# Two transformer blocks on one core: the first half of each layer of the second block in another order

## The chip, the cores and the metric

The kernel runs on 1 core of one Trainium2 chip. The metric is the device time of one execution in microseconds (us), lower is better. Time before: 3315.8 us, the median of 3 runs (3314.15 to 3320.59). Engines are named as in the profile: PE (TensorE), PEld (its weight loads), DVE (VectorE), ACT (ScalarE), POOL (GpSimd), SP (SyncE, which issues the DMAs).

## What is computed

The reference runs `first_block` (a token mixer and a mixture of experts, one layer) and then `second_block`, which has two layers. The change touches the first half of each of these two layers, for 256 tokens of width 1024 in float32:

```python
h = rmsnorm(x, norm_mix[l])
(dq, dk, dv, dz, db, da, sq, sk, sv, iq, ik, iw, xq, gl) = jnp.split(h @ w_in[l], split_pts, axis=-1)
o_dn = deltanet_branch(dq, dk, dv, dz, db, da, conv_w[l], a_log[l], dt_bias[l], dn_norm[l])
o_sa = dsa_branch(sq, sk, sv, iq, ik, iw, positions)
o_xa = memory_branch(xq, rmsnorm(mem, norm_mem[l]), w_mem_kv[l])
# deltanet_branch
qkv = jax.nn.silu(causal_conv(jnp.concatenate([q_in, k_in, v_in], axis=-1), conv_w))
o = gated_delta_rule(q, k, v, beta, g)
o = rmsnorm(o, dn_norm) * jax.nn.silu(z)
# dsa_branch: 8 heads, each query sees the 64 keys with the greatest index score
score = jnp.einsum('bths,bth->bts', jax.nn.relu(jnp.einsum('bthd,bsd->bths', iqb, ik)), iwb)
_, sel = lax.top_k(score, k_sel)
p = jax.nn.softmax(logits, axis=-1)          # over the selected keys
# memory_branch: 4 heads over 256 memory rows
p = jax.nn.softmax(logits, axis=-1)
```

## The kernel before

Every engine has its own program, written out by hand; semaphores tie them together. The two layers are one hardware loop of two rounds (`pe_layers`, `act_layers`, `vec_layers`, `pool_layers`, `sp_layers`).

**Weights.** A layer has 53 weight slabs of 2 MB (`LAY_SLABS`), loaded by SP in that order into three places, slab n into place n mod 3 once the slab before it there is used. Each slab is two halves. A half is split for fp32r products: ACT copies it rounded into a "high" buffer (L1638), DVE subtracts that in place (L1641). `Splitter.until(n, i)` says how far ahead ACT and DVE go: two halves past half i of slab n. The high buffers form rings of three places in SBUF (`RINGS`), so a half can be split only when PE has used the half three before it. PE uses a slab in 96 or 48 matmuls: `project_T` (result transposed, 96 of 256 columns) or `project` (48 of 512 columns), each product in three passes (L451, L452, L453). Results go to four PSUM banks that DVE empties (ring V) or four that ACT empties (ring A); a bank is opened again only when it was emptied.

**Order of the first half of a layer.** PE: 4 slabs of the memory's keys and values; `few` with 16 columns; memory queries xq (slabs 4, 5); the memory's logits (L1830); sq and sk (6 to 9); per memory head a turn of the probabilities (`probs_to_T`, L1806) and the values (L1845); index queries iq (10); `few` with 72 columns; sv (11, 12); transposes of sq, sk, iq, ik; index scores (L1866); six slabs dq, dk, dv of the DeltaNet branch (13 to 18), whose 12 half results ("pairs") ACT copies into `raw` (L2193); own attention: logits of 4 heads (L1876), per head a turn (L1806) and the values (L1898), then the other 4 heads and the norms of q and k by columns of ones (`norms`: L1886, L1890); the DeltaNet solve and the recurrence over 4 chunks (L1920 to L2000); two slabs z (19, 20); gates and branch products (21 and on).

**Convolution.** A pair is convolved in place over its 4 taps: pairs 0 to 8 by DVE (`convolve`, L2469, L2471), one after the split of each slab's half together with one of 8 rounds of taking the 8 greatest scores (L2480 to L2486); pairs 9, 10, 11 by POOL (L2710 to L2715), two blocks each. ACT takes the Silu of the pairs in the order 0 to 11 (L2200), each after a wait for its convolution, and then the exponentials of own attention (`probs`, L2126), which DVE normalises (`normalise`, L2374, L2376).

**After the recurrence.** DVE sums the squares of the result, signals `bgate_free`, POOL takes the power, DVE multiplies by it, by the gain and by Silu(z) (L2592 to L2594) and signals `od_ready`, for which PE waits before it transposes these rows. SP's program, in its queue's order, is: load of slab 21, wait for `bgate_free` (L1699), a DMA of the gate bias (L1700), load of slab 22:

```python
half_spent(sp, l, FIRST[follows(n) + 1] - 1)
load(n, l)
if kind == "in" and at >= GL0 and (at - GL0) % D == 0:
    sp.wait_ge(S("bgate_free"), 3 * l + BRANCHES.index(i) + 1)
    sp.dma_start(bgate, ...)
```

## Time and profile before

| | before |
|---|---|
| median of 3 runs | 3315.8 us |
| profiled execution | 3315.45 us |
| its span in the trace | 3313.6 us |
| PE busy | 2946.2 us (89%) |
| PE weight loads busy | 2303.4 us (70%) |
| DVE busy | 1872.7 us (57%) |
| ACT busy | 1456.6 us (44%) |
| POOL busy | 102.0 us (3%) |
| read from HBM | 608.46 MB |
| mean granted PE clock | 0.940 |

The median, the profiled execution and its span lie within 2.2 us of each other. Busy times are shares of the whole; what the change is worth is read from the stages that it touches. PE counts as busy also where its clock is granted at half speed, so a stage is read by three numbers: its length, PE's idle time and the granted clock.

### The profile page before, as it was taken

What the parts mean: (1) busy time and instruction counts of PE and PEld (TensorE: products, weight loads), DVE (VectorE), ACT (ScalarE), POOL (GpSimd) and SP (SyncE); (2) the same over time, 40 slices, a digit from 0 to 9 for tenths busy, and PEclk for the clock granted to TensorE, in tenths of its full rate; (3) what the DMA queues carried; (4) which work ended last, traced back from release to release, by engine and by line L of the source; (5) the groups of instructions that cost most, each with busy time, mean ns of one, the idle gap of its engine ahead of it and who ended that gap; (6) DMA issues with size and microseconds to landing.
All of it is one profiled execution on the core that took longest, in us unless ns stands there. A gap on an engine that the chain in (4) does not pass through costs nothing.

```text
span 3313.6 us, 41552 instructions
## 1 busy us (share of the span) xinstructions
PE 2946.2 (89%) x15389; PEld 2303.4 (70%) x15389; DVE 1872.7 (57%) x2190; ACT 1456.6 (44%) x1471; POOL 102.0 (3%) x156
## 2 busy tenths in 40 slices
PE   7999898789899989889896799989998958999897
PEld 1345444567666666658786698879797857988896
DVE  1113223788888898885457337545543664365454
ACT  1121111577777777763443435434334333353342
POOL 0000000000000000000004000000000050000000
PEclk9999999899999999998988799989999877999999
DMA  7420331798989888973423004534533320045354
GB/s 295 153 108 26 146 132 52 282 355 341 358 341 355 339 353 341 347 304 140 152 102 128 1 1 153 197 143 161 205 135 127 125 105 1 1 165 209 140 181 181
DMA packets 57721, 611.55 MB, mean 185 GB/s; under 512 B 12603, under 2 KB 18243, under 8 KB 21220
## 3 DMA queue, kind: packets, MB, share of 16 engines
q1 hardware_dynamic: 57574, 609.53, 48.5%
q8 instruction: 99, 1.62, 0.2%
q14 instruction: 48, 0.39, 0.0%
HBM read 608.46 MB, written 1.05 MB: 184 GB/s over the span
## 4 chain that ended last, share of the span: by engine, by line
issue 49%; PE 27%; DVE 9%; DMA 7%; ACT 4%; POOL 3%; DVEq 0%; SPq 0%; POOLq 0%; ACTq 0%
DVE arena_rounded L1225 7%; PE psum_scalar L461 6%; DMA weight_slabs<-in_expert_slabs 5%; PE psum_vector L461 4%; ACT arena_rounded L1222 3%; PE psum_vector L498 3%; PE psum_vector L1278 2%; PE psum_vector L1235 2%; POOL arena L2712 1%; PE psum_scalar L1265 1%; PE psum_scalar L1266 1%; PE psum_vector L451 1%; PE psum_vector L453 1%; PE psum_vector L452 1%; POOL arena L2715 1%
## 5 line engine op out<-in xcount | busy, mean ns | idle before, releaser
L1641 DVE TENSOR_TENSOR weight_slabs_rounded<-weight_slabs,arena_rounded 128x2048 fp32r<-128x2048 f32 x208 | 475.0, 2292 | 484.3 <-ACT arena_rounded L1638 470.3
L1225 DVE TENSOR_TENSOR arena_rounded<-weight_slabs,arena_rounded 128x2048 fp32r<-128x2048 f32 x290 | 651.8, 2288 | 60.1 <-ACT arena_rounded L1222 48.7
L1222 ACT ACTIVATE arena_rounded<-weight_slabs 128x2048 fp32r<-128x2048 f32 x290 | 548.1, 1912 | 128.7 <-DMA weight_slabs<-in_expert_slabs 62.5
L1638 ACT ACTIVATE arena_rounded<-weight_slabs 128x2048 fp32r<-128x2048 f32 x208 | 396.1, 1913 | 405.4 <-PE psum_vector L453 236.3
L451 PE MATMUL psum_vector<-arena_rounded,arena_rounded 128*128 128x512 f32 (+3 forms) x1136 | 404.5, 356 | 28.1 <-DVE weight_slabs_rounded L1641 17.2
L451 PE MATMUL psum_scalar<-arena_rounded,arena_rounded 128*128 128x256 f32 (+1 forms) x1248 | 389.9, 312 | 15.0 <-DVE weight_slabs_rounded L1641 12.1
L1265 PE MATMUL psum_scalar<-arena_rounded,arena_rounded 128*128 128x512 f32 x768 | 320.4, 417 | 74.8 <-DVE arena_rounded L1225 68.5
L1266 PE MATMUL psum_scalar<-arena_rounded,arena_rounded 128*128 128x512 f32 x768 | 304.5, 396 | 0.0
L453 PE MATMUL psum_vector<-arena_rounded,arena_rounded 128*128 128x512 f32 (+2 forms) x784 | 302.5, 386 | 0.0
L452 PE MATMUL psum_scalar<-arena_rounded,arena_rounded 128*128 128x256 f32 x992 | 285.4, 288 | 0.0
L453 PE MATMUL psum_scalar<-arena_rounded,weight_slabs_rounded 128*128 128x256 f32 x992 | 285.0, 287 | 0.0
L452 PE MATMUL psum_vector<-weight_slabs_rounded,arena_rounded 128*128 128x512 f32 x720 | 283.1, 393 | 0.0
L451 PEld LDWEIGHTS psum_scalar<-arena_rounded,arena_rounded 128*128 128x128 f32 x1248 | 245.5, 197 | 28.2 <-ACT small L1477 10.7
L451 PEld LDWEIGHTS psum_vector<-arena_rounded,arena_rounded 128*128 128x128 f32 x1136 | 219.3, 193 | 59.9 <-DVE weight_slabs_rounded L1641 26.5
L1265 PEld LDWEIGHTS psum_scalar<-arena_rounded,arena_rounded 128*128 128x128 f32 x768 | 145.7, 190 | 154.8 <-DVE arena_rounded L1225 127.7
L452 PEld LDWEIGHTS psum_scalar<-arena_rounded,arena_rounded 128*128 128x128 f32 x992 | 195.5, 197 | 0.0
L453 PEld LDWEIGHTS psum_scalar<-arena_rounded,weight_slabs_rounded 128*128 128x128 f32 x992 | 195.3, 197 | 0.0
L461 PE MATMUL psum_scalar<-weight_slabs,arena 128*128 128x512 f32 x416 | 184.7, 605 | 11.7 <-DMA weight_slabs<-in_mixer_slabs 11.7
L453 PEld LDWEIGHTS psum_vector<-arena_rounded,arena_rounded 128*128 128x128 f32 x784 | 152.0, 194 | 29.1
L1309 PE MATMUL psum_vector<-arena_rounded,arena_rounded 128*128 128x512 f32 x384 | 158.3, 412 | 12.3 <-DVE arena_rounded L1225 9.6
L1266 PEld LDWEIGHTS psum_scalar<-arena_rounded,arena_rounded 128*128 128x128 f32 x768 | 146.5, 191 | 26.9
L461 PEld LDWEIGHTS psum_scalar<-weight_slabs,arena 128*128 128x128 f32 x416 | 80.3, 195 | 112.7 <-issue 100.7
(440 smaller groups left out, 4315.1 us busy)
## 6 DMA issues: line engine op xcount, KB each, us to landing
weight_slabs<-in_expert_slabs SPq DMA_DIRECT2D x145, 2048.0 KB, 8.9
weight_slabs<-in_layer_slabs SPq DMA_DIRECT2D x103, 2048.0 KB, 7.8
weight_slabs<-in_mixer_slabs SPq DMA_DIRECT2D x32, 2048.0 KB, 7.9
weight_slabs<-in_layer_slabs SPq DMA_DIRECT2D x6, 1024.0 KB, 5.4
arena<-in_mem SPq DMA_DIRECT2D x3, 1024.0 KB, 9.8
arena<-in_b_gate SPq DMA_DIRECT2D x6, 512.0 KB, 8.1
constants<-in_constants SPq DMA_DIRECT2D x1, 1024.0 KB, 4.9
arena<-in_x SPq DMA_DIRECT2D x1, 1024.0 KB, 7.0
```

Source lines behind the costliest of these rows:

```text
L451: pe.matmul(out, left[0], right[0], start=start, stop=False)
L452: pe.matmul(out, left[0], right[1], start=False, stop=False)
L453: return pe.matmul(out, left[1], right[0], start=False, stop=stop)
L461: mm = pe.matmul(bank[:, :n], hT[:, k, t * P:(t + 1) * P], w[:, k, :n], start=k == 0, stop=k == chunks - 1)
L498: mm = pe.matmul(bank[0:2, :], c2s[:, :, k], w[:, k, :], start=k == 0, stop=k == KC - 1)
L1222: e.activation(high_, whole, ACT.Copy).then_inc(S("expert_high"), 1)
L1225: e.tensor_tensor(low, whole, high_.bitcast(F32), ALU.subtract).then_inc(S("expert_split"), 1)
L1265: pe.matmul(bank, xgT[:, k, :], high[:, k % 4], start=k == 0, stop=False)
L1266: mm = pe.matmul(bank, xgT[:, k, :], low[:, k % 4], start=False, stop=k == KC - 1)
L1309: pe.matmul(banks[side], actT[:, k, :], high[:, k % 2, cols], start=k == 0, stop=False)
L1638: e.activation(fr(high), low, ACT.Copy).then_inc(S("weights_high"), 1)
L1641: e.tensor_tensor(fr(low), low, fr(high).bitcast(F32), ALU.subtract).then_inc(S("weights_split"), 1)
```

## The change

The slabs come in another order, and with them the work of every engine:

- Index queries are slab 4, memory queries 5 and 6, sq 7 and 8, sk 9 and 10, dq/dk/dv 11 to 16, sv 17 and 18; z stays 19 and 20 but is multiplied before the recurrence. Both `few` come together. Index scores are made before sq.
- `take_greatest` (the round of 8) now runs four times beside slabs 9 and 10 and four times beside slabs 12 to 15.
- Convolution: pairs 0, 2, 4, 6, 8 to 11 by DVE, pairs 1, 3, 5, 7 by POOL from pair 1 on. ACT takes the Silus between the copies of later slabs, and all squares of q and k before own attention.
- Own attention: logits of 4 heads, one z slab (in the first group the norms stand between its halves), then turns and values; the same for the other 4 heads. The turns of two heads come ahead of the values.
- The power of Silu(z) is taken once, from SBUF. sq and sk are kept by heads; sq and qT, sk and kT share their places, and other rings are used. SP's program is unchanged but for the slabs' order.

```diff
-LAY_SLABS = ([("mem", BANK * n) for n in range(4)] + [("in", XQ0 + BANK * n) for n in range(2)]
+LAY_SLABS = ([("mem", BANK * n) for n in range(4)] + [("in", IQ0)] + [("in", XQ0 + BANK * n) for n in range(2)]
              + [("in", SQ0 + BANK * n) for n in range(2)] + [("in", SK0 + BANK * n) for n in range(2)]
-             + [("in", IQ0)] + [("in", SV0 + BANK * n) for n in range(2)]
-             + [("in", DQ0 + BANK * n) for n in range(6)] + [("in", DZ0 + BANK * n) for n in range(2)])
+             + [("in", DQ0 + BANK * n) for n in range(6)] + [("in", SV0 + BANK * n) for n in range(2)]
+             + [("in", DZ0 + BANK * n) for n in range(2)])
...
-        RINGS = {0: (112, 120, 48), 13: (72, 80, 24), 19: (48, 56), 21: (48, 56, 136), 35: (112, 120, 88)}
+        RINGS = {0: (112, 120, 48), 11: (112, 120, 24), 19: (112, 120, 96), 21: (48, 56, 136), 35: (112, 120, 88)}
...
-        PAIRS_V = 9
+        BY_VECTOR, BY_POOL = (0, 2, 4, 6, 8, 9, 10, 11), (1, 3, 5, 7)
...
-                ahead = 1 if n in (19, 20) else 2
-                last = min(FIRST[n] + min(i, FIRST[n + 1] - FIRST[n] - 1) + ahead, self.stop - 1)
+                last = min(FIRST[n] + min(i, FIRST[n + 1] - FIRST[n] - 1) + 2, self.stop - 1)
...
+                def own_logits(g):
+                    for h in range(4 * g, 4 * g + 4):
+                        bank = V.open()
+                        for t in range(NT):
+                            mm = pe.matmul(bank[:, t * T:(t + 1) * T], qT[:, h, t * P:(t + 1) * P], kT[:, h, :],
+                                           start=True, stop=True)
+                        V.close(mm)
...
+                V.close(few(V.open(), 16, 72, P))
+                project(V, hT)
                 project_T(A, hT)
...
+                pe.wait_ge(S("index_roped"), l + 1)
+                rows_to_T(pe, A, iq, chunks=4)
+                bank = A.open()
+                for t in range(NT):
+                    mm = pe.transpose(bank[:, t * P:(t + 1) * P], ik[:, t, :], ident)
+                A.close(mm)
                 project_T(A, hT)
+                pe.wait_ge(S("iqT_ready"), l + 1)
+                for h in range(IDXH):
...
+                project(A, hT)
+                probs_to_T(0)
+                probs_to_T(1)
+                project(A, hT)
+                for h in range(XH):
+                    memory_values(h)
+                    if h < 2:
+                        probs_to_T(h + 2)
+                for n in range(6):
+                    project_T(A, hT)
+                    if n == 2:
+                        pe.wait_ge(S("roped"), l + 1)
+                        heads_to_T(sq)
+                        heads_to_T(sk)
+                    own_logits(g)
+                    project(A, hT, norms if g == 0 else None)
+                    at = XH + 4 * g
+                    probs_to_T(at)
+                    probs_to_T(at + 1)
+                    for h in range(4):
+                        own_values(4 * g + h)
+                        if h < 2:
+                            probs_to_T(at + h + 2)
...
-                for n in range(2):
-                    project(A, hT)
...
+                def silu(j):
+                    if j in BY_VECTOR:
+                        e.wait_ge(S("conv_by_vector"), len(BY_VECTOR) * l + BY_VECTOR.index(j) + 1)
                     else:
-                        e.wait_ge(S("conv_by_pool"), (24 - 2 * PAIRS_V) * l + 2 * (j - PAIRS_V) + 2)
+                        e.wait_ge(S("conv_by_pool"), 2 * len(BY_POOL) * l + 2 * BY_POOL.index(j) + 2)
                     step(e.activation(raw[:, 2 * j:2 * j + 2, :], raw[:, 2 * j:2 * j + 2, :], ACT.Silu))
                     e.sem_inc(S("conv_ready"), 1)
+                SILU_AFTER = {2: (0,), 3: (1, 2), 4: (3, 4), 5: (6,)}
+                for n in range(6):
+                    for i in range(2):
+                        weights.until(11 + n, i)
+                        j = 2 * n + i
+                        A.give(e.activation(raw[:, 2 * j:2 * j + 2, :], A.take(), ACT.Copy), wait=True)
+                        e.sem_inc(S("raw_ready"), 1)
+                    if n == 2:
+                        copies([qT[:, k:k + 2, :] for k in range(0, KC, 2)] + [kT[:, k:k + 2, :] for k in range(0, KC, 2)])
+                        signal("qkT_ready")
+                    for j in SILU_AFTER.get(n, ()):
+                        silu(j)
+                for n in range(2):
+                    weights.until(17 + n)
+                    for t in range(NT):
+                        A.give(e.activation(sv[:, t, n * BANK:(n + 1) * BANK], A.take(), ACT.Copy))
+                    for j in ((5, 8, 9), (7, 10, 11))[n]:
+                        silu(j)
+                for part, squared_ in enumerate((q_squares, k_squares)):
+                    for j in range(0, H2, 2):
+                        step.go(e.activation(squared_[:, j:j + 2, :], raw[:, H2 * part + j:H2 * part + j + 2, :], ACT.Square))
+                step.sync()
+                e.sem_inc(S("squares_ready"), 1)
...
                     for h in range(4 * g, 4 * g + 4):
+                        if h % 2 == 0:
+                            weights.until(19 + g, h % 4 // 2)
+                        e.wait_ge(S("rmax_ready"), 12 * l + XH + h + 1)
                         probs(h, 1.0)
+                    for t in range(NT):
+                        A.give(e.activation(zrow[:, t, g * BANK:(g + 1) * BANK], A.take(), ACT.Copy))
+                    prob_turned(4 * g)
+                    prob_turned(4 * g + 1)
                     for h in range(4 * g, 4 * g + 4):
                         A.give(e.activation(osT[:, h, :], A.take()[:, 0:T], ACT.Copy))
+                        if h % 4 < 2:
+                            prob_turned(h + 2)
...
+                weights.upto(FIRST[21] + 1)
+                A.given()
+                step(e.activation(zrow, zrow, ACT.Silu))
+                e.sem_inc(S("z_ready"), 1)
...
+                for i in range(2):
+                    weights.until(10, i)
+                    take_greatest()
...
+                for n in range(4):
+                    weights.until(12 + n, 0)
+                    convolve(BY_VECTOR[n])
+                    weights.until(12 + n)
+                    take_greatest()
                 step(ts(barred, work, -2e38, NEG, ALU.is_gt, ALU.mult))
+                for n in range(2):
+                    for i in range(2):
+                        weights.until(16 + n, i)
+                        convolve(BY_VECTOR[4 + 2 * n + i])
+                weights.until(18)
...
+                own_greatest(0)
+                for h in range(4):
+                    if h == 2:
+                        weights.until(19, 0)
+                    normalise(h, XH + h)
...
-                for b in range(2 * PAIRS_V, 24):
+                for b in [2 * j + i for j in BY_POOL for i in range(2)]:
...
```

The new order on the engines, as a listing of their programs has it (in brackets the semaphores that an instruction waits for).

ACT before, after the last copies of the six DeltaNet slabs (L2193): Silus (L2200), then the exponentials (L2126).

```order
L2193 ACTIVATE arena<-psum_scalar 128x512 [waits lay_scalar_free,lay_scalar_full]
...
L2200 ACT_TABLE_LOAD
L2200 ACTIVATE arena<-arena 128x512 [waits conv_by_vector]
...
L2200 ACTIVATE arena<-arena 128x512 [waits conv_by_pool]
L176 REGISTER_ALU
L2199 REGISTER_ALU [waits lay_scalar_step]
L2200 ACTIVATE arena<-arena 128x512 [waits conv_by_pool]
...
L2126 ACT_TABLE_LOAD
L2126 ACTIVATE arena,small<-arena,small 128x256 [waits rmax_ready]
```

ACT now, from the end of the DeltaNet slabs (L2259 are its copies, L2269 those of sv, L2251 Silus, L2274 squares, L1639 high copies).

```order
L2259 ACTIVATE arena<-psum_scalar 128x512 [waits lay_scalar_full]
...
L2251 ACTIVATE arena<-arena 128x512 [waits lay_scalar_free,conv_by_pool]
...
L2269 ACTIVATE arena<-psum_scalar 128x512 [waits lay_scalar_full] x2
L2250 REGISTER_ALU
L2251 ACTIVATE arena<-arena 128x512 [waits conv_by_pool]
...
L2251 ACTIVATE arena<-arena 128x512 [waits conv_by_vector]
...
L2274 ACTIVATE arena<-arena 128x512 [waits lay_scalar_step]
L2274 ACTIVATE arena<-arena 128x512 x7
...
L2163 ACTIVATE arena,small<-arena,small 128x256 [waits rmax_ready]
```

The Silus moved between copies; the wait for POOL's last pair (7) now stands behind the copies of sv and ahead of the squares.

PE before, at the second group of own attention (L1876 logits, L1886 and L1890 norms, L1806 a turn, L1898 values).

```order
L1876 MATMUL psum_vector<-arena 128x256
L200 REGISTER_ALU [waits g_ready,squares_ready]
L1886 MATMUL psum_vector<-constants,arena 128x1 [waits lay_vector_free]
...
L1890 MATMUL psum_vector<-small,constants 128x8 x4
L1893 REGISTER_ALU
L200 REGISTER_ALU [waits prob_ready]
L1806 MATMUL psum_scalar<-constants,arena 128x128 [waits lay_scalar_free]
```

PE now, at the first group, between the halves of z slab 19 (L1858 and L1863 norms).

```order
L453 MATMUL psum_scalar<-arena_rounded_66,arena_rounded_53 128x512
L200 REGISTER_ALU [waits g_ready,squares_ready]
L1858 MATMUL psum_vector<-constants,arena 128x1 [waits lay_vector_free]
...
L1863 MATMUL psum_vector<-small,constants 128x8 x4
L1723 REGISTER_ALU
L451 MATMUL psum_scalar<-arena_rounded_67,arena_rounded_54 128x512 [waits weights_split]
```

A z slab's matmuls now stand between the logits and the first turn.

ACT now, behind the recurrence's copies (L2335); before, the copies of z stood here and the high copies of slabs 20 and 21 between them.

```order
L2335 ACTIVATE arena<-psum_scalar 64x512 [waits lay_scalar_full]
L228 REGISTER_ALU
L2338 ISA [waits lay_scalar_free]
L1635 REGISTER_ALU [waits bgate_free]
L1639 ACTIVATE arena_rounded_69<-weight_slabs 128x2048 [waits lay_slab1]
```

The first half that ACT prepares here is now slab 22's (place 1), where it was slab 20's.

## Rows read from the trace of the kernel before

**Rows 1.** The page: busy time per engine, granted clock in 40 slices.

```profile
PE 2946.2 (89%) x15389; PEld 2303.4 (70%) x15389; DVE 1872.7 (57%) x2190; ACT 1456.6 (44%) x1471; POOL 102.0 (3%) x156
...
PEclk9999999899999999998988799989999877999999
```

**Rows 2.** Waits of PE, first layer, 1553.2 to 1877.9: total, times, longest.

```profile
PE psum_scalar L1806 <- DVEq L2378: 40.4, 2, 36.2
PE psum_scalar L1898 <- ACTq L2214: 12.4, 8, 6.7
PE psum_scalar L1845 <- ACTq L2174: 5.1, 4, 2.6
```

**Rows 3.** Timeline, all engines, about the longest wait: start, duration, [idle before <- releaser].

```profile
1776.03 2.29 DVE L1641 TENSOR_TENSOR weight_slabs_rounded<-weight_slabs,arena_rounded 128x2048 fp32r<-128x2048 f32 x1
1777.84 0.53 POOL L2706 TENSOR_TENSOR arena<-halves 128x1 f32<-128x1 f32 x1 [263.57 <-ACTq L2194]
...
1786.24 0.19 POOL L2710 TENSOR_TENSOR small<-halves 128x1 f32<-128x1 f32 x1 [0.18 <-POOL arena L2715]
...
1802.36 0.19 POOL L2710 TENSOR_TENSOR small<-halves 128x1 f32<-128x1 f32 x1 [0.18 <-POOL arena L2715]
...
1816.88 0.19 POOL L2710 TENSOR_TENSOR small<-halves 128x1 f32<-128x1 f32 x1 [0.18 <-POOL arena L2715]
...
1823.17 0.72 POOL L2715 TENSOR_TENSOR arena<-arena 128x256 f32<-128x256 f32 x1
1823.97 0.63 ACT L2200 ACTIVATE arena<-arena 128x512 f32<-128x512 f32 x1 [13.82 <-POOLq L2716]
...
1827.23 0.17 DVE L2374 RECIPROCAL small<-small 128x2 f32<-128x2 f32 x1 [15.72 <-ACTq L2129]
...
1828.24 1.11 PE L1806 MATMUL psum_scalar<-constants,arena 128*128 128x128 f32 x4 [36.17 <-DVEq L2378]
```

**Rows 4.** Windows: length, busy (instructions) of PE, PEld, DVE, ACT, POOL, then PEclk, DMA.

```profile
1553.20:1788.40 235.20, 220.79 (x1355) 199.13 (x1354) 129.79 (x240) 91.86 (x103) 9.74 (x16) 0.93 0.37 135
1788.40:1878.00 89.60, 41.05 (x180) 34.06 (x179) 36.21 (x92) 31.20 (x70) 32.26 (x52) 0.62 0.06 24
...
1997.80:2020.00 22.20, 22.08 (x97) 17.94 (x96) 12.91 (x12) 9.51 (x9) 2.93 (x1) 1.00 0.33 119
...
2453.00:2690.00 237.00, 223.04 (x1347) 201.24 (x1347) 129.58 (x239) 91.36 (x103) 9.48 (x16) 0.91 0.37 134
2690.00:2780.00 90.00, 41.45 (x180) 33.92 (x180) 36.46 (x93) 31.19 (x70) 32.55 (x52) 0.60 0.07 24
```

**Rows 5.** Windows: own attention after the long wait; DeltaNet slabs; after a late pause.

```profile
1828.20:1878.00 49.80, 37.39 (x162) 31.17 (x163) 14.41 (x42) 18.46 (x50) 0.00 (x0) 0.63 0.00 1
...
1740.00:1780.00 40.00, 40.00 (x336) 40.00 (x335) 33.77 (x67) 15.68 (x13) 2.01 (x5) 1.00 0.48 170
...
2150.00:2205.00 55.00, 41.58 (x198) 35.29 (x197) 28.18 (x35) 17.41 (x15) 0.70 (x1) 0.84 0.36 134
```

**Rows 6.** Groups of DVE, 1733 to 1777 (POOL idle): count | busy, mean ns.

```profile
L1641 DVE TENSOR_TENSOR weight_slabs_rounded<-weight_slabs,arena_rounded 128x2048 fp32r<-128x2048 f32 x9 | 20.6, 2292 | 5.5 <-ACT arena_rounded L1638 4.8
L2471 DVE SCALAR_TENSOR_TENSOR arena<-arena,small 128x254 f32<-128x254 f32 (+2 forms) x24 | 10.5, 481 | 0.4
```

**Rows 7.** The same, 1784.9 to 1802.55 (POOL convolving beside it).

```profile
L2471 DVE SCALAR_TENSOR_TENSOR arena<-arena,small 128x254 f32<-128x254 f32 (+2 forms) x18 | 9.9, 590 | 0.3
```

**Rows 8.** Waits and timeline of the DMA queue on SP, 1780 to 2010.

```profile
SPq L1699 <- DVEq L2584: 212.2, 1, 212.2
...
2001.68 0.33 SPq L1700 DMA_DIRECT2D arena<-in_b_gate  x1
2009.25 34.14 SPq L1658 DMA_DIRECT2D weight_slabs<-in_layer_slabs  x4
```

**Rows 9.** The page: ACT's high copy in the layers, and a slab's load.

```profile
L1638 ACT ACTIVATE arena_rounded<-weight_slabs 128x2048 fp32r<-128x2048 f32 x208 | 396.1, 1913 | 405.4 <-PE psum_vector L453 236.3
...
weight_slabs<-in_layer_slabs SPq DMA_DIRECT2D x103, 2048.0 KB, 7.8
```

368 lines of the change are left out of this document (176 added, 192 removed).

## The prediction

> **What bounds the kernel now.** I read the page first: PE is busy for 89% of the span at a mean clock of 0.94, and the slices in which both fall are two, one in each layer of the second block [rows 1]. Then the waits of PE over one layer's first half: of 64 us idle one wait is 36.2 us, that of the first turn of own attention for DVE's normalised probabilities [rows 2]. Then the timeline behind that wait, read backwards [rows 3]: PE starts at 1828.24, behind DVE's normalising at 1827.23, behind ACT's exponentials, which follow ACT's last Silu at 1823.97; that Silu waited 13.8 us for POOL, whose last add is at 1823.17. POOL began only at 1777.84, when pair 9 was there, and had six blocks to do. So a wait that is booked on DVE is POOL's convolution, handed on by ACT's fixed order. Last the windows [rows 4], to see what the stage is worth. The part up to the last DeltaNet slab takes 235.2 us with 220.8 busy at clock 0.93; own attention takes 89.6 us with 41.1 busy at 0.62; the two z slabs, behind the recurrence, take 22.2 us at full clock without a pause. The second layer reads the same: 237.0, 223.0 at 0.91, and 90.0, 41.5 at 0.60.
>
> **The ledger.** The change moves work within these 235.2 + 89.6 + 22.2 = 347.0 us per layer and takes none of PE's work away: the same matmuls are issued. So I count losses against PE's work. Before: idle 235.2 - 220.8 = 14.4 and 89.6 - 41.1 = 48.6; slow clock 0.07 x 220.8 = 15.5 in the first part, and 0.37 x 37.4 = 13.8 behind the long wait, where the clock is 0.63 [rows 4, 5]. That is 92 us lost, and 255 us of work per layer at full clock. Everything hangs on what is lost afterwards.
>
> **The change, part by part**, with T0 the start of the first DeltaNet slab and T the end of sv. A slab takes 96 x 40.0 / 336 = 11.4 us transposed and 22.2 / 2 = 11.1 us by rows [rows 4, 5]; T is T0 + 6 x 11.4 + 4 for the transposes of sq and sk + 22 = T0 + 95.
>
> - *Index scores and both small products early.* Same instructions. The score of a head costs an ACT copy and two DVE operations, and PE has four banks for eight heads, so it waits about 2 us; the next slab goes to the other ring, so DVE's sums are hidden behind sq. The memory's values find their banks behind ACT's copies of sk, about 2 us more. With turns of two heads ahead, the waits per memory head (5.1 us) [rows 2] should be nearly gone. Idle: 4 taken; 2 at the least, 14.4 as before at the most. The clock is granted slow after thin matmuls and after such waits; I take 12 of the 15.5, between 5 and 15.5.
> - *DVE in the DeltaNet slabs.* Before, one slab cost it two splits, a convolution and a round of eight: 33.8 us busy in 40 at PE's full pace [rows 5], 9.6 per slab of 11.4. Slabs 12 to 15 carry just that now, but with POOL beside them: the taps took 481 ns alone and 590 ns beside POOL [rows 6, 7], which adds 0.7 per pair, and a wait of up to 0.9 per split. That is 12.1 at the most, 0.7 over. Slabs 16 and 17 have two convolutions and no round, 4.6 + 2 x 4 to 2 x 4.5, so up to 2.2 over each. Lag 7 at the worst, against a lead of two halves (11.4) less copy and split (1.9 + 2.3), which is 7 [rows 6, 9]. I take 3; 0 and 12 are the ends.
> - *POOL.* It now has eight blocks, from T0 + 11.5. A block took (1802.36 - 1786.24) / 2 = 8.1 us beside DVE's taps and (1816.88 - 1802.36) / 2 = 7.3 later [rows 3]. No split ran beside it but one: POOL's first operation, 1777.84 to 1778.37, lasted 0.53 where its like takes 0.19, and ended 0.05 after the split that ran from 1776.03 to 1778.32. So I let a split hold POOL, for some 1.8 us, twice a slab: POOL works 7.8 us in 11.4, a block takes 8.1 x 11.4 / 7.8 = 11.8, and pair 7 is done at T0 + 106 = T + 11. Unheld it would be T0 + 76.
> - *Own attention.* ACT takes Silu 7 at T + 11, then pairs 10 and 11 and eight squares (0.6 each): squares ready at T + 18. PE does the logits (to T + 3.6), waits 1 us for z's first half, whose high buffer is that of sv's last half, and is through it at T + 10. It waits 8 us for the squares, does 9 us of norms (my estimate) and z's second half. The softmax of four heads (by my estimate 12 us through DVE and ACT, with two high copies between) is hidden behind these. Then turns and values, twice; before they cost 12.4 us of waits [rows 2], 6.7 of them for ACT's first copy behind its squares; 4 taken. The second group's softmax is covered by logits and z slab, 14.7. Idle 1 + 8 + 4 = 13, between 5 and 35; if POOL ends by T the 8 are gone. Clock: the norms' thin matmuls and the pause were slow before, 13.8; I take 12, between 5 and 15.
> - *z moved ahead.* Its 22.2 us are in the ledger. But they covered something. SP may not load slab 22 before `bgate_free`, which came at 2001.68, 3.9 us after the recurrence's last matmul [rows 8, 4]; before, slabs 19, 20 and 21 lay ready by then. Now only 21 does, 11.1 us of work, to 2008.9 on the old times. Slab 22 is issued at 2002, lands at about 2010.5 (7.8 us, behind the bias) [rows 9], is copied (1.9) and split (2.3): ready at 2014.8, PE waits 6. Behind that the first branch slab's split stands behind DVE's work on the DeltaNet rows and the first gate sums: 3. A late pause costs clock too (0.84 over 55 us around two waits) [rows 5]: 3. Tail: 12, between 4 and 22, z's whole length.
> - One Silu of z from SBUF, the rope by heads, fewer table changes: hidden in ACT and DVE, 0; if their cover goes it is the lag above.
>
> Sum of losses: 4 + 12 + 3 + 13 + 12 = 44, and 12 in the tail. Gain 92 - 44 - 12 = 36 per layer, 72 for both. The profiled execution took 3315.45, which is the median (3315.8) within 0.4. **Forecast: 3315.5 - 72 = 3243 us.** About 0.2% is what a measurement of this kernel can tell from no change.
>
> **The rivals.**
>
> - *The losses are smaller*: POOL is not held, so the squares are early; slab 22 comes in time; the clock stays up. Losses 28, tail 12 gives 52 per layer, **3211**; with a tail of 5 as well, 3197. For it: DVE's work beside POOL slowed POOL's blocks only from 7.3 to 8.1. Against: the one split seen beside POOL did hold it.
> - *DVE becomes the bound* of the DeltaNet slabs, lag 12 for 3: 27 per layer, **3261**. For it: 84% busy there already, and one of its operations is slower beside POOL. Against: two halves of lead.
> - *POOL is held by every operation of DVE's in turn*, not by splits alone: of a block's seven operations each waits for what DVE has in hand. With 0.5 us for each of seven taps and the two splits, a block comes to about 15 us, pair 7 to T0 + 131, and PE waits 25 us longer: 11 per layer, **3293**. Against: with DVE busy over 80% with taps and rounds, a block took 8.1. The Trainium skill's page "SBUF — State Buffer", section "Who interferes with whom", states this lock: VectorE and GpSimd share a port pair, an operation of VectorE with two SBUF inputs contends with a GpSimd read, and whichever starts second is blocked until the first ends. By that rule the trace agrees on the split that held POOL; it also speaks against sharing the convolution between these two engines over the whole DeltaNet stage.
> - *Slower than before*: the same chain, longer. ACT's order is fixed: behind the wait for pair 7 stand the squares, the exponentials and the high copies that PE needs. The gain of 36 is used up when pair 7 is 36 us later, at T0 + 142, a block of (142 - 11.5) / 8 = 16.3 us, twice what was measured. At 18.5 us a block the wait is 54 longer, 18 per layer lost, **3351**. Against it: while PE stands still DVE runs out of splits, and POOL catches up.
> - *The change doesn't do what it says*: the order of the programs shows z between logits and turns and the pairs shared; I leave this nothing of its own.
>
> **How the numbers follow.** Forecast 0.54, smaller losses 0.22, DVE 0.12, POOL held in turn 0.08, slower 0.04. All but the last are faster by over 0.2% (7 us); I move 0.02 from POOL's case and 0.01 from DVE's to no change: faster 0.93, same 0.03, slower 0.04. The bounds of single terms (clock 5 to 15 in each part, tail 4 to 22) move the forecast by some 20 per layer either way if several go together. The range leaves out the far half of the smaller losses and the slower case: 3205 to 3290.
>
> **What would show it.** Right: no wait of PE over 12 us in a layer's first half; POOL busy from the second pair on, its last add within 15 us of the end of sv; PE's wait before the norms 5 to 10 us; between first DeltaNet slab and the end of sv some 100 us; after the recurrence a wait of about 6 us before slab 22, for a split whose load was issued behind the gate bias. Wrong: waits for splits of 3 us or more all through the DeltaNet slabs (DVE's case), blocks of POOL of 15 us (held in turn), or a granted clock near 0.6 again in own attention, which would say that the pauses were only cut into pieces.

## The result, and the profile after

| | before | changed |
|---|---|---|
| median | 3315.7 us (4 runs, 3314.15 to 3320.59) | 3219.4 us (4 runs, 3212.26 to 3227.25) |
| ratio | | 0.9708, 95% interval 0.9682 to 0.9734 |
| profiled execution, span | 3315.45, 3313.6 | 3216.56, 3214.7 |
| mean granted PE clock | 0.940 | 0.956 |

The kernel is 2.9% faster, 96 us. The forecast was 72 (3243 us); the time lies inside the range, on its fast side. The page of the changed kernel, the rows that answer to [rows 1]:

```profile
PE 2932.7 (91%) x15389; PEld 2301.2 (72%) x15389; DVE 1873.0 (58%) x2162; ACT 1458.6 (45%) x1473; POOL 173.7 (5%) x200
...
PEclk9999999799999999999899899989998999999999
```

The work is the same, 15389 matmuls. POOL has eight blocks per layer for six and is busy 72 us longer in all, and nobody waits longer for it. No slice of the layers stands at clock 0.7 any more. Now the windows, to be held against [rows 4]; columns as there. They are the first narrow product to the end of sv, own attention with both z slabs, the DeltaNet solve and recurrence, and slabs 21 and 22 with 16 transposes up to the start of slab 23, all in the first layer; then the first two for the second layer:

```profile
1554.20:1781.80 227.60, 218.05 (x1356) 198.38 (x1355) 146.33 (x266) 98.25 (x112) 77.84 (x89) 0.95 0.38 139
1781.80:1840.90 59.10, 56.08 (x275) 47.98 (x274) 28.41 (x59) 34.12 (x69) 0.00 (x0) 0.88 0.10 36
1840.90:1963.30 122.40, 116.20 (x985) 112.78 (x982) 55.08 (x95) 49.65 (x92) 0.00 (x0) 0.97 0.01 1
1963.30:1997.10 33.80, 26.05 (x115) 21.04 (x113) 20.25 (x16) 14.43 (x12) 2.93 (x1) 0.90 0.57 217
...
2404.00:2635.00 231.00, 221.49 (x1374) 201.50 (x1373) 147.23 (x267) 101.09 (x114) 77.84 (x89) 0.96 0.38 139
2635.00:2692.00 57.00, 53.98 (x268) 46.34 (x267) 27.80 (x60) 31.99 (x70) 0.00 (x0) 0.88 0.07 31
```

The last two stretches of the first layer in the kernel before, the DeltaNet part and the end of the z slabs to the start of slab 23:

```profile
1878.00:1997.80 119.80, 115.64 (x984) 112.16 (x982) 53.18 (x93) 46.49 (x90) 0.00 (x0) 0.99 0.01 1
2019.90:2044.40 24.50, 23.69 (x113) 19.77 (x113) 21.37 (x18) 14.81 (x11) 0.00 (x0) 1.00 0.50 178
```

What took 347.0 us takes 227.6 + 59.1 = 286.7, which is 60.3 less. Two stretches give some of that back. Slabs 21 and 22 with their transposes took 24.5 us and take 33.8, 9.3 more. The DeltaNet part took 119.8 us and takes 122.4, 2.6 more: its first wait, for the factors, is 5.0 us for 2.6. That is 60.3 - 9.3 - 2.6 = 48.4 us per layer, and twice that is 96.8, against the 98.9 by which the spans differ. The ledger closes within about 2 us.

The waits of PE, 1553 to 1841, to be held against [rows 2]:

```profile
PE psum_scalar L451 <- ACT arena L2154: 5.1, 1, 5.1
PE psum_scalar L1817 <- ACT arena L2238: 2.6, 1, 2.6
PE psum_scalar L451 <- DVE weight_slabs_rounded L1642: 2.3, 3, 1.0
PE psum_vector L1858 <- ACTq L2276: 1.3, 1, 1.3
PE psum_scalar L1837 <- ACTq L2229: 0.8, 2, 0.4
PE psum_scalar L451 <- ACT arena L2228: 0.4, 1, 0.4
```

Instead of 64 us there are 12.5. The waits of the turns and values, 12.4 + 5.1 = 17.5 us before, have come down to the rows of L1817, L1837 and L2228, 3.8. The wait for the squares (L1858), for which the forecast had 8, is 1.3. New at the top is a wait of 5.1 for ACT at L2154. The timeline of all engines at the squares shows why POOL costs nothing:

```profile
1779.49 0.84 POOL L2824 TENSOR_TENSOR arena<-arena 128x256 f32<-128x256 f32 x1
...
1781.86 3.71 ACT L1639 ACTIVATE arena_rounded<-weight_slabs 128x2048 fp32r<-128x2048 f32 x2 [10.29 <-PE psum_scalar L453]
...
1786.43 0.63 ACT L2251 ACTIVATE arena<-arena 128x512 f32<-128x512 f32 x1
...
1788.75 4.28 ACT L2274 ACTIVATE arena<-arena 128x512 f32<-128x512 f32 x8
...
1793.20 3.73 PE L1858 MATMUL psum_vector<-constants,arena 128*128 128x1 f32 x32 [1.27 <-ACTq L2276]
```

POOL's last add ends at 1780.33. ACT comes for that pair (L2251) only at 1786.43: it stood for 10.29 us for PE's last sv slab and then had two high copies to make. So POOL is done 6 us before it is asked for.

### The profile page after: what moved, and what is told of

Its sections match the earlier page's. It is cut to its first block, busy times and chain, and to the rows that moved or that the text cites. A ratio compares the mean times of both kernels' runs of the same rounds, so it can differ in the third digit from the quotient of the medians.

```text
span 3214.7 us, 41574 instructions
## 1 busy us (share of the span) xinstructions
PE 2932.7 (91%) x15389; PEld 2301.2 (72%) x15389; DVE 1873.0 (58%) x2162; ACT 1458.6 (45%) x1473; POOL 173.7 (5%) x200
## 4 chain that ended last, share of the span: by engine, by line
issue 45%; PE 30%; DVE 9%; DMA 7%; POOL 5%; ACT 4%; DVEq 0%; SPq 0%; POOLq 0%; ACTq 0%
DVE arena_rounded L1225 7%; PE psum_scalar L461 6%; DMA weight_slabs<-in_expert_slabs 5%; PE psum_vector L461 4%; ACT arena_rounded L1222 3%; PE psum_vector L498 3%; PE psum_vector L1278 2%; POOL arena L2821 2%; PE psum_vector L1235 2%; PE psum_scalar L1265 2%; POOL arena L2824 2%; PE psum_scalar L1266 1%; PE psum_vector L451 1%; PE psum_vector L453 1%; PE psum_vector L452 1%
## 5 line engine op out<-in xcount | busy, mean ns | idle before, releaser
L1642 DVE TENSOR_TENSOR weight_slabs_rounded<-weight_slabs,arena_rounded 128x2048 fp32r<-128x2048 f32 x208 | 478.4, 2308 | 419.9 <-ACT arena_rounded L1639 403.2
L1639 ACT ACTIVATE arena_rounded<-weight_slabs 128x2048 fp32r<-128x2048 f32 x208 | 396.2, 1913 | 451.2 <-PE psum_vector L453 260.0
L451 PE MATMUL psum_vector<-arena_rounded,arena_rounded 128*128 128x512 f32 (+3 forms) x1136 | 411.1, 362 | 41.5 <-DVE weight_slabs_rounded L1642 31.2
L451 PEld LDWEIGHTS psum_vector<-arena_rounded,arena_rounded 128*128 128x128 f32 x1136 | 224.5, 198 | 75.7 <-DVE weight_slabs_rounded L1642 41.2
L451 PEld LDWEIGHTS psum_scalar<-arena_rounded,arena_rounded 128*128 128x128 f32 x1248 | 243.4, 195 | 45.2 <-ACT arena L2154 10.6
L453 PEld LDWEIGHTS psum_vector<-arena_rounded,arena_rounded 128*128 128x128 f32 x784 | 156.6, 200 | 29.8
```

The source lines that it names most:

```text
L451: pe.matmul(out, left[0], right[0], start=start, stop=False)
L453: return pe.matmul(out, left[1], right[0], start=False, stop=stop)
L1639: e.activation(fr(high), low, ACT.Copy).then_inc(S("weights_high"), 1)
L1642: e.tensor_tensor(fr(low), low, fr(high).bitcast(F32), ALU.subtract).then_inc(S("weights_split"), 1)
```

## The experiments

All are edits of the changed kernel. Six undo or worsen parts of the change, to see what each is worth (1 to 6); three take away one wait each that is left, and one has these together (7 to 10); two are about the clock (11, 12). Ratios are to the kernel before, with 95% intervals; the changed kernel stands at 0.9708, and 0.001 of ratio is 1.66 us per layer.

**1. POOL starts late again (pool_last).**

```diff
-        BY_VECTOR, BY_POOL = (0, 2, 4, 6, 8, 9, 10, 11), (1, 3, 5, 7)
+        BY_VECTOR, BY_POOL = (0, 1, 2, 3, 4, 5, 6, 7, 8), (9, 10, 11)
```

ACT's Silus follow this order, and DVE takes its ninth pair (8) behind the splits of the last sv slab.

> Edit of the changed kernel: POOL takes pairs 9, 10 and 11 of the convolution (as before the change) and VectorE pairs 0 to 8; everything else stays in the new order. Theory A (the gain is a sum of parts; sharing the convolution from its second half-slab on is one of them): POOL starts some 44 us later, at the tenth pair, and has 6 blocks of 7 to 10.4 us, so it ends 41 to 62 us after that, 12 to 23 us behind the end of the last sv slab instead of 1.5 us ahead of it. The squares come 12 to 20 us later, TensorE waits for them ahead of the norms for 13 to 21 us instead of 1.3, and the kernel takes 12 to 20 us more per layer, 24 to 40 in all (3243 to 3259). Rival 1 (the split of the convolution carries nearly the whole gain): about 45 us per layer, over 3300. Rival 2 (the softmax of the own attention hides POOL anyway): under 5 us per layer, below 3230.

Measured: 3261.04 us, ratio 0.9840 (0.9822 to 0.9857), 22 us more per layer, just above the 20 expected. The first layer, timeline about the squares:

```profile
1804.04 0.72 POOL L2825 TENSOR_TENSOR arena<-arena 128x256 f32<-128x256 f32 x1
1804.84 0.63 ACT L2251 ACTIVATE arena<-arena 128x512 f32<-128x512 f32 x1 [11.81 <-POOLq L2826]
1805.59 4.26 ACT L2274 ACTIVATE arena<-arena 128x512 f32<-128x512 f32 x8
1810.03 6.98 PE L1858 MATMUL psum_vector<-constants,arena 128*128 128x1 f32 x32 [20.20 <-ACTq L2276]
```

The chain of [rows 3] is back: POOL, a Silu of ACT that waits 11.8 us for it, the squares, and PE, which waits 20.2 instead of 1.3. The 32 narrow products behind that wait take 6.98 us where they took 3.73: the rest of the 22 us is clock. Sharing from the first pairs on carries almost half the gain, by removing this chain; rivals 1 and 2 fall.

**2. POOL made slower (pool_plus).**

```diff
                         step.go(e.tensor_tensor(unused, halves[:, 0:1], halves[:, 0:1], ALU.mult))
+                        if tap == 2:
+                            step(e.tensor_scalar(slack[:, 0, late:T], raw[:, b, 0:T - late], tap_column(tap, b), None, ALU.mult))
+                            step.go(e.tensor_tensor(unused, halves[:, 0:1], halves[:, 0:1], ALU.mult))
```

> Edit of the changed kernel: each of POOL's eight blocks gets one more multiplication of 255 columns (its result goes to a cell that nobody reads) and one more of its small dummy operations, about 1.65 us per block, 13 us per layer. Theory A (POOL now ends 1.5 us ahead of the sv slabs, ScalarE comes for its last pair 4.6 us behind their end): POOL ends about 11.7 us behind the sv slabs, the last silu and all squares come 7 us later, TensorE waits for them about 8 us instead of 1.3, and the kernel takes 5 to 9 us more per layer, 10 to 18 in all (3229 to 3237). Rival (POOL's end is still covered, as own logits and the first half of a z slab lie before the norms): under 2 us per layer. Rival 2 (POOL is the bound now, all of its added time shows): 13 us per layer, 3245.

Measured: 3235.7 us, ratio 0.9763 (0.9747 to 0.9779), 9 us more per layer. POOL's last add ends 11.1 us behind the start of the own logits instead of 1.3 ahead of it, and ACT now waits for it:

```profile
1793.94 0.72 POOL L2828 TENSOR_TENSOR arena<-arena 128x256 f32<-128x256 f32 x1
1794.74 0.63 ACT L2252 ACTIVATE arena<-arena 128x512 f32<-128x512 f32 x1 [6.28 <-POOLq L2829]
...
1801.49 6.98 PE L1859 MATMUL psum_vector<-constants,arena 128*128 128x1 f32 x32 [7.53 <-ACTq L2277]
```

Of 12.4 us by which POOL ends later, 6.3 are on PE's path and 6 were slack; with the clock behind it the step costs 9. So POOL has a slack of 6 us, behind which each us costs more than one. This is the mechanism of the "slower than before" case, at the point where it begins.

**3. The z slabs behind own attention (z_behind).**

```diff
                     own_logits(g)
-                    project(A, hT, norms if g == 0 else None)
+                    if g == 0:
+                        norms()
...
+                for g in range(2):
+                    project(A, hT)
+
                 def tile(t):
```

> Edit of the changed kernel: the two z slabs are multiplied between the own attention and the DeltaNet recurrence instead of between each group's logits and its turns; the norms keep their place after the first group's logits. Theory A: in the first group the norms themselves (11 to 14 us) cover the softmax, but TensorE gets to them 6 to 8 us before the squares and waits that long; in the second group nothing covers it: four heads of 1.86 us on VectorE, an exponential and a division, 8 to 10 us of waiting. With 2 to 4 us of half clock that is 15 to 22 us per layer, 30 to 44 in all (3249 to 3263). Rival 1 (z slabs are the whole gain): 45 us per layer, over 3300. Rival 2 (groups of four are enough by themselves): under 5 us per layer.

Measured: 3249.27 us, ratio 0.9802 (0.9784 to 0.9821), 15.6 us more per layer. The waits of PE in the same stretch:

```profile
PE psum_vector L1858 <- ACTq L2280: 7.9, 1, 7.9
PE psum_scalar L1817 <- DVEq L2457: 5.8, 1, 5.8
```

The z slabs' copies on ACT move with them. Both waits stand where theory A put them, 7.9 us ahead of the norms and 5.8 in the second group. The second was expected at 8 to 10 and is smaller. They are 12.4 us more than in the changed kernel, the waits for z's first split and the first values 1.7 less; the other 5 are clock: turns that take 1.0 us there take 2.0 here.

**4. Turns directly ahead of the values (turns_late).**

```diff
-                    probs_to_T(at)
-                    probs_to_T(at + 1)
                     for h in range(4):
+                        probs_to_T(at + h)
                         own_values(4 * g + h)
-                        if h < 2:
-                            probs_to_T(at + h + 2)
```

and the same for the memory's heads and for ACT's order.

> Edit of the changed kernel: in the memory and the own attention each head's probabilities are turned directly before its values again, not two heads ahead, and ScalarE's copies follow that order. Theory A: TensorE then waits 0.8 to 1.3 us for ScalarE's copy at each of the 12 heads, 10 to 15 us per layer, 20 to 30 in all (3239 to 3249). Rival (other work on ScalarE set these times already): no difference over 5 us in all.

Measured: 3247.05 us, ratio 0.9803 (0.9785 to 0.9821), 15.7 us more per layer, just over the band. The waits:

```profile
PE psum_scalar L1828 <- ACTq L2223: 7.8, 4, 5.2
PE psum_scalar L1837 <- ACTq L2223: 6.6, 8, 0.9
```

Eleven heads wait 0.8 to 0.9 us each. One waits 5.2: the first of the memory, because ACT, at the end of the second sk slab, first makes two high copies (3.7 us) and the two copies of sk (1.1 us). That is 10.6 us more of waits, and 5 of clock. Turning ahead is worth as much as the z slabs.

**5. All three at once (undone).**

> The edits of three runs together: POOL takes the last three pairs, the z slabs follow the own attention, and turns stand directly ahead of their values. What is left of the change is the early index scores, the order of the slabs, the groups of four and the transposes in place. Alone, the three cost 0.0132, 0.0094 and 0.0095 of the time before. Theory A (each part pays for a wait of its own at its own place: the squares, the second group's softmax, the copy of the turned probabilities): they add up, 0.999 to 1.006 of the time before, which is the whole gain and a little more. Rival 1 (they cover one and the same chain of the own attention, so that the second undone costs less): 0.980 to 0.992. Rival 2 (the early index scores and the new order carry a gain of their own, so that even this kernel is faster than before by over 0.5 per cent).

Measured: 3330.38 us, ratio 1.0051 (1.0035 to 1.0068): 0.5% slower than before the change. The single ratios add up to 0.9708 + 0.0132 + 0.0094 + 0.0095 = 1.0029, and the three add up within the intervals. The waits of PE, first layer:

```profile
PE psum_vector L1858 <- ACTq L2271: 26.9, 1, 26.9
PE psum_scalar L1828 <- ACTq L2227: 7.7, 4, 5.2
PE psum_scalar L1837 <- ACTq L2227: 6.5, 8, 0.8
PE psum_scalar L1817 <- DVEq L2445: 5.1, 1, 5.1
```

Each wait is the one of its own run (L1817 is 5.1 for 5.8), and the first is the sum of two: 1.3 + 18.9 (late POOL) + 6.6 (z no longer ahead of the norms) = 26.8. And the windows of the same two parts (here both z slabs are within the second):

```profile
1554.20:1787.00 232.80, 219.97 (x1344) 199.59 (x1344) 140.28 (x266) 95.84 (x108) 29.63 (x36) 0.93 0.37 136
1787.00:1898.20 111.20, 72.75 (x277) 59.85 (x276) 33.31 (x67) 36.14 (x72) 24.02 (x32) 0.66 0.05 20
```

The first narrow product starts at 1553.31 here, so the two parts take 344.9 us. Between the same points, 1553.23 to 1877.83 and the z slabs' 22.2 us, the kernel before took 346.8. So early index scores, the new order of slabs, groups of four and transposes in place together give no more than 2 us per layer. The later stretches still cost their price: the tail, where slab 22 is still late, takes 34.0 us for 24.5, and the DeltaNet part 123.8 for 119.8. That is why this kernel is behind the one before. Theory A holds; both rivals fall.

**6. Index scores late (index_late).** Turned between the two sk slabs, multiplied behind the memory attention, and all eight rounds beside the convolution:

```diff
+                pe.wait_ge(S("iqT_ready"), l + 1)
+                for h in range(IDXH):
...
                 for n in range(6):
                     project_T(A, hT)
...
                     weights.until(12 + n)
                     take_greatest()
+                    take_greatest()
```

> Edit of the changed kernel: the index queries are turned between the two sk slabs and the index scores are multiplied behind the memory attention, directly ahead of the DeltaNet slabs; all eight rounds of the greatest scores stand beside the convolution, two behind each of four pairs. Theory A: TensorE loses the 5.06 us wait at the early place, but VectorE gets 6 to 7 us of scores and four more rounds of 1.82 us (7.3 us) in the 97 us of the DeltaNet slabs, in which its splits, eight pairs and four rounds already fill about 80: the splits run behind and TensorE waits for them, a net loss of 3 to 12 us per layer, 6 to 24 in all, 0.9726 to 0.978 of the time before. Rival (VectorE has room for it, and only the 5 us wait shows): 5 us per layer gained, 0.968.

Measured: 3214.81 us, ratio 0.9694 (0.9671 to 0.9718). The interval holds the changed kernel's 0.9708 and the rival's 0.968, and leaves out all of theory A's range: my theory falls, and the rival stands, with 2.3 us per layer for its 5 and not told from no gain. PE's waits for splits grow from 2.3 to 4.1 us and the early wait falls from 5.1 to 0.9; DVE had the room that I denied it. The early place of the index scores has no part in the gain that these runs can tell.

**7. The gates' small activations later (bat_later).** This is about the wait of 5.06 us that is new. What ACT did meanwhile, in the timeline of the changed kernel:

```profile
1595.61 0.60 ACT L2199 ACTIVATE arena<-psum_scalar 128x512 f32<-128x512 f32 x1 [3.36 <-PE psum_scalar L453]
1596.22 1.28 ACT L2204 ACT_TABLE_LOAD   x1
1597.52 0.22 ACT L2204 ACTIVATE small<-small 128x16 f32<-128x16 f32 x1
1597.75 1.28 ACT L2205 ACT_TABLE_LOAD   x1
...
1599.39 1.28 ACT L2207 ACT_TABLE_LOAD   x1
...
1601.10 1.09 ACT L2154 ACTIVATE arena<-psum_scalar 128x512 f32<-128x512 f32 x2 [0.19 <-ACT small L2207]
```

Four operations of 0.2 us, with three table loads, stand ahead of the copies that free PE's banks. The edit moves them behind the ReLUs:

```diff
-                e.wait_ge(S("bat_ready"), l + 1)
-                step.go(e.activation(beta, bat[:, :, 0:H2], ACT.Sigmoid, scale=-1.0))
...
-                e.sem_inc(S("softplus_ready"), 1)
                 copies([iqT[:, k:k + 2, :] for k in range(0, 4, 2)])
```

> Edit of the changed kernel: ScalarE's four small activations of the gates (sigmoid, exponential twice, logarithm, with three table loads, 4.7 us) stand behind the eight ReLUs of the index scores instead of ahead of the copies of the turned index queries. Theory A: these four cause the one wait of 5.06 us that TensorE has in the early part (for ScalarE's copy of the index queries), and part of the half clock behind it: 5 to 7 us less per layer, 10 to 14 in all; against the changed kernel's 0.9708 of the time before that is 0.9666 to 0.9678. Rival (the wait only moves: VectorE's queries or ScalarE's exponentials of the memory attention come 4.7 us later and TensorE waits for them): within 3 us of the changed kernel.

Measured: 3207.52 us, ratio 0.9668 (0.9649 to 0.9687), 6.6 us less per layer. The wait is gone, and from the last turn of the index keys to the last index product it is 18.3 us instead of 25.2.

**8. The load of slab 22 ahead of the bias (bias_behind).** The tail of the changed kernel: SP's queue, ACT's copy and DVE's split of slab 22, and PE:

```profile
1967.20 0.33 SPq L1701 DMA_DIRECT2D arena<-in_b_gate  x1
1967.87 26.74 SPq L1659 DMA_DIRECT2D weight_slabs<-in_layer_slabs  x4
```

```profile
1976.73 1.91 ACT L1639 ACTIVATE arena_rounded<-weight_slabs 128x2048 fp32r<-128x2048 f32 x1 [12.69 <-DMA weight_slabs<-in_layer_slabs]
...
1978.67 2.29 DVE L1642 TENSOR_TENSOR weight_slabs_rounded<-weight_slabs,arena_rounded 128x2048 fp32r<-128x2048 f32 x1 [11.86 <-ACT arena_rounded L1639]
...
1981.02 0.80 PE L451 MATMUL psum_vector<-arena_rounded,arena_rounded 128*128 128x512 f32 x1 [6.50 <-DVE weight_slabs_rounded L1642]
```

```diff
-                    if kind == "in" and at >= GL0 and (at - GL0) % D == 0:
+                    if kind == "in" and at >= GL0 and (at - GL0) % D:
```

> Edit of the changed kernel: on SyncE's queue the load of the gate's second slab (22, 26, 30) goes ahead of the wait for the bias buffer and of the bias load, for all three gates. Theory A: slab 22 has its place free since the own attention, so it lands long before it is wanted; TensorE's wait of 6.5 us behind slab 21 goes, and the half clock behind it (7 us at half speed, 3.5 lost): 6 to 10 us less per layer, 12 to 20 in all, 0.9648 to 0.9672 of the time before. Rival 1 (the bias comes later and VectorE waits for it instead, since its load now stands behind a slab of 9 us): no gain, or up to 3 us per layer lost. Rival 2 (slab 23 is late next): half the gain.

Measured: 3206.25 us, ratio 0.9673 (0.9657 to 0.9689), 5.8 us less per layer. The 6.5 us wait is gone: slabs 21 and 22 run in one piece of 22.1 us. What is left in the tail is the wait behind slab 22, 1.2 us, as before the edit. The window of the tail, to be held against the changed kernel's 33.80 us at 0.90:

```profile
1965.70:1990.90 25.20, 23.95 (x115) 19.77 (x113) 20.24 (x16) 14.45 (x12) 2.94 (x1) 1.00 0.60 208
```

In the tail 8.6 us came back, the wait and 2 us of clock. The whole gained 5.8, just below the 6 expected. In this execution the part ahead of the tail took 3 us longer than in the changed kernel's, with the same waits of PE but a lower clock (0.94 for 0.95 up to the end of sv, 0.86 for 0.88 in own attention). Whether that comes from the edit or from the difference between any two executions is not shown.

**9. The factors earlier (logs_early).** ACT's Ln moves behind the first group's exponentials, DVE's seven small operations ahead of the second group, ACT's Exp of the factors behind the first group's values, and DVE's memsets behind its last division:

```diff
+                    if g == 0:
+                        e.wait_ge(S("norms_ready"), l + 1)
+                        step(e.activation(nrm, nrm, ACT.Ln))
+                        e.sem_inc(S("norm_logs_ready"), 1)
                     for t in range(NT):
                         A.give(e.activation(zrow[:, t, g * BANK:(g + 1) * BANK], A.take(), ACT.Copy))
```

> Edit of the changed kernel: the logarithm of the norms is taken by ScalarE behind the first group's exponentials, VectorE's seven small operations on it stand ahead of the second group's greatest values, the exponential of the factors behind the first group's values, and VectorE's two memsets of the state (0.9 us each) behind the last division; before, all of it stood behind the own attention, where TensorE waits 4.97 us for the factors and then runs 6.9 us at half clock. Theory: both engines are idle for 8 to 11 us where these operations go, so the wait goes and 2 to 3.5 us of clock with it: 5 to 8.5 us less per layer, 10 to 17 in all, 0.9657 to 0.9678 of the time before. Rival (what the DeltaNet part waits for next, the decays and tiles on VectorE, only takes the wait over): under 3 us in all.

Measured: 3207.08 us, ratio 0.9673 (0.9657 to 0.9689), 5.8 us less per layer. The changed kernel had, at the start of the DeltaNet part,

```profile
1847.63 0.79 PE L1965 MATMUL psum_scalar<-arena_rounded 128*128 128x512 f32 x1 [4.97 <-ACTq L2299]
```

and in this run the same line has no wait, and takes 0.48 us for 0.79. The kernel before waited 2.6 us at this place, so half of the wait was new with the change.

**10. The three together (three).**

> The edits of the three other runs of this call together. They lie at three places of the layer that share no wait, so theory A adds them up: 32 to 51 us below the changed kernel, 0.9554 to 0.9612 of the time before. Rival (they share a resource, the clock or ScalarE): less than two thirds of the sum of the three.

Measured: 3179.94 us, ratio 0.9587 (0.9568 to 0.9605). The three single gains sum to 0.0040 + 0.0035 + 0.0035 = 0.0110; together they are 0.0121. They add up, within the intervals.

**11. The second narrow product behind a wide slab (three_few).** DVE takes the results in the new order too.

```diff
                 V.close(few(V.open(), 0, 16, 16))
-                V.close(few(V.open(), 16, 72, P))
                 project(V, hT)
+                V.close(few(V.open(), 16, 72, P))
```

> The run of the three edits together with one more: the second narrow product of 72 columns stands behind the slab of the index queries and not directly behind the first of 16 columns. The two lie in one stretch of half clock of 17.1 us now. Theory: one narrow product between wide ones is too short for the clock to fall as far, so that 3 to 6 us per layer come back, 6 to 12 in all: 0.955 to 0.957 of the time before against 0.9587. Rival (the clock falls just as long, twice, or the index keys and weights come later and TensorE waits for them at the turns): within 3 us of the run without it, or slower.

Measured: 3170.05 us, ratio 0.9562 (0.9538 to 0.9585). The difference of 0.0025 alone is within the intervals; the windows over the same three products, first without and then with the edit, show it:

```profile
1555.40:1585.20 29.80, 29.80 (x146) 27.22 (x145) 7.98 (x25) 4.31 (x3) 0.00 (x0) 0.71 0.19 71
```

```profile
1550.50:1576.90 26.40, 26.40 (x146) 23.82 (x144) 6.53 (x8) 6.23 (x4) 0.00 (x0) 0.81 0.37 130
```

The same 146 matmuls take 3.4 us less, all of it clock, 0.71 to 0.81. The 72 columns ran in 5.4 us instead of 10.4, and the 16 columns ahead of them took 7.7 for 6.4.

**12. The norms in two pieces (norms_split).** The second tile's narrow products go behind z's second half; the query squares move to a place that is free by then, and ACT takes the logarithm of the norms behind the first group's values.

```diff
                     project(A, hT, norms if g == 0 else None)
+                    if g == 0:
+                        norms((1,))
```

> The four edits together (0.9562 of the time before) with one more: the norms' narrow products of the first tile stay between the halves of the z slab, those of the second tile go behind its second half; the query squares lie where the own values go later (free by then), and ScalarE's logarithm of the norms moves behind the first group's values. Now the norms take 16.4 us in one piece of which the first tile's 6.2 us of one-column products, then 7.0 for the same number at half clock, and the half slab behind them 8.1 instead of 5.7 us; at full clock one tile takes 3.7 + 1.5 us. Theory (a narrow stretch of 5 us between wide products does not pull the clock down, as the run before showed for the 72 columns): 4 to 8 us less per layer, 8 to 16 in all, 0.951 to 0.954 of the time before. Rival 1 (the idle 2.2 us and one tile's narrow products are enough for the clock to fall, and it falls twice): no gain. Rival 2 (the later logarithm makes TensorE wait for the factors again): up to 3 us per layer lost.

Measured: 3167.55 us, ratio 0.9567 (0.9551 to 0.9582): no difference. The windows of the norms' second piece and of the turns and values behind it:

```profile
1795.30:1800.70 5.40, 5.40 (x42) 5.40 (x41) 0.00 (x0) 0.60 (x1) 0.00 (x0) 0.79 0.77 273
1800.70:1808.60 7.90, 7.90 (x34) 6.44 (x35) 3.17 (x8) 3.55 (x7) 0.00 (x0) 0.71 0.20 81
```

The clock falls a second time, in the turns and values behind the second piece, 0.71 where the run before had 1.00. Norms, half slab, norms, turns and values take 7.8 + 7.3 + 5.4 + 7.9 = 28.4 us and took 30.4 with the norms in one piece, so 2 us came back in this layer, which the time of the whole doesn't tell. Rival 1 is the nearest.

## Why the prediction was right, and where its sizes were off

The sign, the mechanism and the places of the waits were as forecast; the gain is 48 us per layer for 36, a third more than forecast. Terms missed in both directions, but most of the difference is one stage. By the terms:

| term of the sum, per layer | forecast | measured |
|---|---|---|
| idle up to the end of sv (early 4, lag of DVE 3) | 7 | 227.6 - 218.05 = 9.6 |
| idle in own attention | 13 | 59.1 - 56.08 = 3.0 |
| slow clock up to the end of sv | 12 | 0.05 x 218.05 = 10.9 |
| slow clock in own attention | 12 | 0.12 x 56.08 = 6.7 |
| tail | 12 | 33.8 - 24.5 = 9.3 |
| DeltaNet part | left out of the sum | 122.4 - 119.8 = 2.6 |

**The step that failed is that of own attention**, 25 forecast for 9.7 measured, and in it two terms.

- *"PE waits 8 us for the squares"*. It rested on a block of POOL of 11.8 us. A block took (1780.33 - 1697.26) / 8 = 10.4, so pair 7 was done at T - 1.5 and not at T + 11. Of the signs named, this is the one that did not come: a wait of 5 to 10 us before the norms. The lock itself was seen rightly: beside two splits of DVE, POOL's rows read

```profile
1740.11 2.40 DVE L1642 TENSOR_TENSOR weight_slabs_rounded<-weight_slabs,arena_rounded 128x2048 fp32r<-128x2048 f32 x1
1740.91 2.19 POOL L2824 TENSOR_TENSOR arena<-arena 128x254 f32<-128x254 f32 x1
...
1744.39 0.73 POOL L2824 TENSOR_TENSOR arena<-arena 128x253 f32<-128x253 f32 x1
...
1747.04 2.53 DVE L1642 TENSOR_TENSOR weight_slabs_rounded<-weight_slabs,arena_rounded 128x2048 fp32r<-128x2048 f32 x1 [0.23 <-DVE arena L2579]
1747.60 2.02 POOL L2819 TENSOR_TENSOR small<-halves 128x1 f32<-128x1 f32 x1 [0.18 <-POOL arena L2824]
```

An add of 0.73 takes 2.19 and ends 0.6 behind the split; a small operation of 0.19 takes 2.02 and ends 0.05 behind it. POOL lost about 1.5 and 1.8 us. All 12 splits that DVE made while POOL worked held one of its operations like this, for 1.5 to 2.1 us, 20.8 us in all. So the hold of some 1.8 us per split was right. Two other numbers were too large. The splits came one per 6.9 us (12 in 83.1) and not one per 5.7: there was none for 8.4 us beside the transposes of sq and sk. And a block without its holds took (83.1 - 20.8) / 8 = 7.8 us, where 8.1 was taken. The rule that was cited for this, the Trainium skill's "SBUF — State Buffer", section "Who interferes with whom", is borne out by these rows; what I drew from it, that it speaks against letting the two engines share this stage, is not: with POOL from the second pair on, held as it is, the kernel is 22 us per layer faster than with POOL beginning at pair 9.

- *"Then turns and values, twice; 4 taken"*. 0.8 us is what the own attention shows (L1837). Two turns ahead are enough to hide a copy of 0.6 us.

**The clock followed**: with 1.3 us of pause ahead of the norms there was less of it to lose, 6.7 for 12, a term that I had taken over from the kernel before. The first 32 products of the norms take 3.73 us, and 6.98 in pool_plus and pool_last, behind pauses of 7.5 and 20.2.

*Early idle* was forecast too small, 4 for 8.1 (5.1, 2.6 and 0.4 in the waits above). I had looked for it in PE's banks and overlooked what the move does on ACT: three table loads now stand ahead of copies that PE waits for, 5.06 us (experiment 7). The order of ACT's program had them there to be read.

*The lag of DVE* was forecast at 3 and is 1.4, in two waits of at most 1.0 (the third of L1642 is at z's first half). *The tail* came by the mechanism worked out, and 9.3 for 12 in size: slab 22 is issued behind the bias at 1967.87, copied at 1976.73, split by 1981.0, and PE waits 6.5 for 6; the second wait is 1.2 for 3, and the clock took 0.10 x 26.05 = 2.6 for 3. *The DeltaNet part* was left out of the ledger as unchanged; its wait for the factors grew from 2.6 to 5.0. The rival of DVE as the bound is excluded by these waits, and by experiment 6, which put four more rounds and the scores on DVE in the same stretch for 1.8 us of waits. The case of smaller losses (3211) came nearest in time, with early squares, but not for the reason it gave: POOL was held at every split, and the squares were early all the same.

## What to carry to other kernels

When a wait is booked on one engine, follow the order of each engine's program back until an operation is found that began late; here a convolution on POOL that began late, because its pairs came last, was booked as TensorE's wait for VectorE. Independent small covers (a slab of other work, turning two heads ahead, an earlier start of the slowest engine) each pay for a wait of their own, and add up; undone singly, they show which part of a large reordering does the work; here the early index scores, the first item on the list of changes, did none that the runs can tell. After a move, read what now stands ahead of it on every queue it passes: three table loads and one wait ahead of a bias load cost 12 us per layer (bat_later and bias_behind), and three such edits with one more (three_few, 3170.05 us, ratio 0.9562) beat the changed kernel by another 1.5%.

## What the runs showed of the hardware beyond this

- The clock was lower behind a pause and thin work: 0.63 behind the 36 us wait before the change, 0.88 in the same stage with 3 us of pauses. And an equal amount of narrow work is not equally dear: 48 products of 72 columns took 10.4 us directly behind 48 of 16 columns, and 5.4 behind a wide slab (three and three_few); with what the products around them lost, 3.4 us were left of these 5. Cut in two (norms_split), narrow work made the clock fall in the stretch behind it instead.
- A wait cost more than itself in these runs: 20.2 us behind POOL cost 22 per layer for 18.9 us of added wait, the 6.3 us of pool_plus cost 9, and the 10.7 net of z_behind 15.6. Taking away 6.5 us (bias_behind) gave 8.6 in its stretch, though 5.8 in the whole.
- A switch of ACT's tables costs 1.30 us here: the load takes 1.28 and the next operation begins 0.02 behind it, while the load begins 0.01 to 0.02 behind the operation before. The Trainium skill's page "ScalarE: Activation LUTs", section "What ACT_TABLE_LOAD costs", gives 1.283 us for the load, as here, and 1.38 us of drain beside it, which these rows don't show.
